# A two-block transformer forward on one core: the first shift and scale in three stages

## The chip, the cores and the metric

The kernel runs on one core of a Trainium2 chip. Time is device microseconds (us) of one execution. A core has TensorE (PE; its weight loads are listed apart as PEld), VectorE (DVE), ScalarE (ACT), GpSimd (POOL) and SyncE (SP), which here only issues transfers.

## The reference, cut to what matters

Two blocks follow each other on 256 tokens of width 1024. Everything is float32. The change touches only the start of the first block's first layer:

```python
cs = jax.nn.silu(c)
for layer in range(DEPTH):
    mod = cs @ ada_w[layer] + ada_b[layer]            # 1024 x 3072
    shift, scale, gate = jnp.split(mod, 3, axis=-1)
    h = rms_norm(x, norm_g[layer]) * (1.0 + scale[:, None, :]) + shift[:, None, :]
    ...
    y = even_mixer(h, ...)                            # first: proj = h @ w_in
    x = x + gate[:, None, :] * y
```

So shift and scale, 2048 columns of one vector times ada_w, must be there before h, and h before the first product with w_in.

## The kernel before

**Slots.** All weights stand in HBM as slots of 128 partitions by 2048 floats (1 MB). NAMES (`plan`) lists them in the order in which TensorE uses them; IDX is a name's place there. SyncE issues their transfers in the order LOADS, into a ring of four buffers (`ring`) and three more (in `big2`); a transfer into a used buffer waits until `slot_done`, which counts the slots that TensorE has finished, has passed the buffer's last user. The first slots are ada0_0 to ada0_7 (shift and scale of layer 0), then even0, even2, even4, even1, even3, even12 (EVEN_FIRST: column blocks of w_in, 256 columns each).

**An ada slot** holds 512 columns of ada_w for half of the depth (4 of 8 chunks of 128 rows). `pe_slot` multiplies it with cs, chunk by chunk, in four groups of 32 columns of the array, 16 instructions of 128 columns; two slots make one bank of PSUM. `dve_mod_slot` reduces a bank in four steps to eight columns, of which `dve_mod` makes mod: shift (columns 0 to 7, one per chunk of h) and 1 + scale times norm_g (8 to 15).

**Split products.** A product with w_in is made of three in float32r: high weights by high h, high weights by the rest of h, rest of the weights by high h. A slot's high part is a cast on ScalarE into `w_split` (two buffers, `act_highs`), its rest a subtraction on VectorE back into the ring (`dve_lows`). h has eight chunks: `hh` (high, VectorE), `hT` (full, ScalarE) and `hT_r` (the rest, VectorE). `scr` is x over its root mean square. A slot takes 3 x 16 instructions.

**The head.** TensorE (block of L2386) multiplies ada0_0 and ada0_1, then sums the squares of x (`pe_row_squares`), then the other ada slots, with `pe_turning` between and behind them: products of constants that nothing reads. Then `pe_first_pair` multiplies even0 and even2, in the order: high by high for both, the rest of even0 by high, high of even0 by the rest of h (even0 ends), high of even2 by the rest, the rest of even2 (even2 ends). All other slots follow in order by `pe_slot`. ScalarE (L2479) squares x, takes the root, casts even0 and even2 in halves, makes hT, and then `act_slot` for each name: it empties the slot's bank, then makes the high part of the slot two behind, which needs the `w_split` buffer of the slot that has just ended. VectorE (L2588) makes scr and mod, hh, the rests.

Every engine runs its own list in order. A signal of `s` is counted by who posts it and taken by who waits.

## Time and profile before

| | us |
|---|---|
| median of 3 runs (1266.88 to 1285.79) | 1268.56 |
| profiled execution | 1268.02 |
| its span, first to last instruction | 1266.2 |
| TensorE busy | 1241.9 (98%) |
| VectorE busy | 828.0 (65%) |
| ScalarE busy | 684.1 (54%) |
| moved by DMA | 222.91 MB, mean 176 GB/s |

Busy is the time in which an engine worked on an instruction; a matmul instruction on float32 leaves two records, one on float32r leaves one. Register, branch and semaphore work is not counted. The times of the views count from the span's start.

### The profile page before, as it was taken

To read this page: it belongs to the slowest core of one execution; us is meant where nothing else is said; L and a number is where in the kernel's file an instruction comes from. 1 tells how busy PE (TensorE), PEld (TensorE's weight loads), DVE (VectorE), ACT (ScalarE), POOL (GpSimd) and SP (SyncE) were. 2 spreads that over 40 slices of the span, in tenths; PEclk is the share of its full clock that TensorE was granted. 3 is DMA by queue.
4 is the path that set the end of the run, shared out by engine and by line. 5 is a ranking of instruction groups with operands and counts; after the bars stand their busy time and mean duration, and the time that the engine had idled before them with its cause. 6 is when DMAs were issued, how large, how long until landed. Compare 5 with 4: busy or idle time off the path is not lost.

```text
span 1266.2 us, 24533 instructions
## 1 busy us (share of the span) xinstructions
PE 1241.9 (98%) x10376; PEld 1123.4 (89%) x10376; DVE 828.0 (65%) x1239; ACT 684.1 (54%) x886; POOL 99.1 (8%) x83
## 2 busy tenths in 40 slices
PE   6999999999999999999999999999999999999998
PEld 5998899879999999899888888999999999888886
DVE  3667856886866969766655545766868857555533
ACT  2556446765756567245544435756567345544433
POOL 0000000000000430230000000000430130000000
PEclk9999999999999999999999999999999999999999
DMA  9867665624544433225555554544442325555552
GB/s 383 299 259 277 253 232 189 259 100 160 168 140 167 167 134 134 70 101 176 190 172 194 185 185 168 168 159 164 152 152 101 102 100 183 177 190 189 176 170 96
DMA packets 35101, 222.91 MB, mean 176 GB/s; under 512 B 3888, under 2 KB 8240, under 8 KB 9264
## 3 DMA queue, kind: packets, MB, share of 16 engines
q1 hardware_dynamic: 31104, 215.97, 48.5%
q10 hardware_dynamic: 3888, 5.38, 1.3%
q8 instruction: 82, 1.34, 0.4%
q14 instruction: 27, 0.22, 0.0%
HBM read 220.28 MB, written 1.05 MB: 175 GB/s over the span
## 4 chain that ended last, share of the span: by engine, by line
PE 93%; DVE 3%; DMA 2%; ACT 1%; issue 1%; SPq 0%; POOL 0%; ACTq 0%; DVEq 0%
PE pj L637 62%; PE yv L637 14%; PE sc L637 10%; PE tp L637 4%; DVE ring_rounded L751 1%; PE tp L503 1%; DMA ring<-weights 1%; DMA xT<-x_t 1%; PE tp L2003 1%; DVE att_area L580 1%; ACT att_area L534 0%; ACT probsT L1669 0%; DVE att_area L605 0%; ACT w_split L742 0%; DVE big L1876 0%
## 5 line engine op out<-in xcount | busy, mean ns | idle before, releaser
L751 DVE TENSOR_TENSOR ring_rounded<-ring,w_split 128x2048 fp32r<-128x2048 f32 x106 | 248.2, 2347 | 59.5 <-ACT w_split L742 57.3
L2240 DVE TENSOR_TENSOR ring_rounded<-ring,big_rounded 128x2048 fp32r<-128x2048 f32 x66 | 151.3, 2293 | 107.4 <-ACT big_rounded L2116 107.2
L742 ACT CAST w_split<-ring 128x2048 fp32r<-128x2048 f32 x106 | 202.2, 1908 | 31.8 <-PE pj L637 22.5
L637 PE MATMUL pj<-h_split,w_split 128*128 128x256 f32 x1264 | 172.1, 286 | 0.2 <-ACT w_split L2498 0.2
L637 PE MATMUL pj<-h_split,ring_rounded 128*128 128x256 f32 x1264 | 165.3, 281 | 1.3 <-DVE ring_rounded L751 1.3
L637 PEld LDWEIGHTS pj<-h_split,w_split 128*128 128x128 f32 x1264 | 156.2, 189 | 6.3 <-issue 5.1
L637 PEld LDWEIGHTS pj<-h_split,ring_rounded 128*128 128x128 f32 x1264 | 155.7, 188 | 2.9 <-DVE ring_rounded L751 2.1
L2116 ACT CAST big_rounded<-ring 128x2048 fp32r<-128x2048 f32 x66 | 126.2, 1911 | 50.2 <-PE pj L637 44.8
L637 PE MATMUL pj<-hT_rounded,w_split 128*128 128x256 f32 x1136 | 146.0, 280 | 0.0
L637 PEld LDWEIGHTS pj<-hT_rounded,w_split 128*128 128x128 f32 x1136 | 139.2, 188 | 0.0
L637 PE MATMUL sc<-big_rounded 128*128 128x512 f32 x176 | 67.8, 391 | 0.0
L637 PE MATMUL pj<-big_rounded 128*128 128x512 f32 x176 | 67.5, 389 | 0.0
L2340 ACT ACTIVATE big<-pj 128x512 f32<-128x512 f32 x32 | 19.1, 598 | 67.5 <-PE pj L637 67.4
L534 ACT ACTIVATE att_area<-att_area,stat 128x256 f32<-128x256 f32 (+1 forms) x80 | 39.9, 499 | 19.4 <-DVE stat L580 8.3
L2125 ACT CAST big_rounded<-tp 128x512 fp32r<-128x512 f32 x22 | 12.9, 588 | 69.1 <-PE tp L2003 69.1
L637 PE MATMUL yv<-big_rounded,yT_rounded 128*128 128x512 f32 x192 | 49.2, 398 | 0.1
L637 PE MATMUL yv<-big_rounded,rw_rounded 128*128 128x512 f32 x192 | 47.7, 390 | 0.0
L637 PE MATMUL yv<-ring_rounded,yT_rounded 128*128 128x512 f32 x192 | 47.5, 389 | 0.0
L1425 POOL TENSOR_TENSOR big<-big 128x512 f32<-128x512 f32 x16 | 30.7, 1919 | 200.0 <-DVE big L1341 189.7
L637 PEld LDWEIGHTS yv<-ring_rounded,yT_rounded 128*128 128x128 f32 x192 | 36.0, 188 | 7.5
L637 PEld LDWEIGHTS yv<-big_rounded,rw_rounded 128*128 128x128 f32 x192 | 35.9, 188 | 7.4
L637 PEld LDWEIGHTS yv<-big_rounded,yT_rounded 128*128 128x128 f32 x192 | 35.0, 188 | 8.1 <-issue 0.8
(379 smaller groups left out, 2127.2 us busy)
## 6 DMA issues: line engine op xcount, KB each, us to landing
ring<-weights SPq DMA_DIRECT2D x180, 1024.0 KB, 4.9
big<-weights SPq DMA_DIRECT2D x20, 1024.0 KB, 7.8
first_block<-biases ACTq DMA_DIRECT2D x26, 192.0 KB, 4.4
first_block<-biases SPq DMA_DIRECT2D x6, 192.0 KB, 10.8
xT<-x_t SPq DMA_DIRECT2D x1, 1024.0 KB, 9.7
con<-constants SPq DMA_DIRECT2D x1, 897.0 KB, 6.6
aux<-small SPq DMA_DIRECT2D x1, 832.0 KB, 10.9
out_t<-scr SPq DMA_DIRECT2D x3, 256.0 KB, 2.4
```

Source lines behind the costliest of these rows:

```text
L503: last = nc.tensor.transpose(tp[m["t"] % 2][:, at:at + P], probs[:, m["g"] % 4, it, jt * P:(jt + 1) * P], C("ident"))
L534: ins = nc.scalar.activation(pr, pr, ACT.Exp, bias=st[:, it:it + 1], scale=-1.0, accum_out=st[:, 2 + it:3 + it])
L580: ins = nc.vector.tensor_tensor_reduce(probs[:, m["g"] % 4, it, 0:size], sc[m["g"] % 2][:, it * SEQ:it * SEQ + size], table[:, P - it * P: ...
L637: return nc.tensor.matmul(out, lhsT, rhs, start=start, stop=stop, skip_group_check=True)
L742: act.post(nc.scalar.copy(w_split[:, w % 2], ring[:, in_ring(idx)]), s["w_high"])
L751: dve.post(nc.vector.tensor_tensor(ring_r[:, at], ring[:, at], w_split[:, w % 2].bitcast(F32), ALU.subtract), s["w_low"])
L1425: pool.tell(nc.gpsimd.tensor_tensor(d, b, b[:, :, n - 1:n].to_broadcast([P, 512 // (2 * n), 2 * n]), ALU.subtract), s["hgrn_diff"])
L2003: last = nc.tensor.transpose(tp[j % 2][:, (2 * c + T) * P:(2 * c + T + 1) * P], by_token(j, T)[:, c * P:(c + 1) * P], C("ident"))
L2116: act.tell(nc.scalar.copy(w_high(i), ring[:, in_ring(w_at(t, i))]), s["ffn_high"])
L2125: act.tell(nc.scalar.copy(hidden_high(j), tp[j % 2][:, :]), s["ffn_placed"])
L2240: dve.tell(nc.vector.tensor_tensor(w_low(t, i), w, value(w_high(i)), ALU.subtract), s["ffn_low"])
L2340: free(act, nc.scalar.activation(GATES[name], b[:, :], ACT.Tanh, scale=0.5), name)
```

## The change

The list of the first slots is now ada0_0, ada0_1, ada0_4, ada0_5 (shift and scale of the first four chunks of h), four new slots, and EVEN_FIRST. A new slot, a quarter, holds 256 columns of ada_w over the full depth: ada0_22 and ada0_26 are shift and scale of chunks 4 and 5, ada0_23 and ada0_27 those of chunks 6 and 7. `pe_quarter` multiplies one with 32 instructions of 64 columns into a bank `yv`; `dve_quarters` reduces a pair of them in four steps. The transfers are in the order of HEAD_ORDER: vec, x_t, the constants, four ada slots, even0, even2, and then the four quarters. h and the products of even0 and even2 are made in three stages of 4, 2 and 2 chunks, with the quarters between them. The squares stand ahead of all ada slots, and the nine turnings behind ada0_5 are gone; the twelve ahead of the pair stay.

```diff
-HEAD_BUFFERS = [RING + i for i in range(OWN)] + list(range(RING)) + [RING]
+HEAD_BUFFERS = [RING, RING + 1, RING + 2, 0, 3, RING, RING + 1, RING + 2]
+HEAD_ORDER = [0, 1, 2, 3, 8, 9, 4, 5, 6, 7]
+HEAD_MODS = ("ada0_0", "ada0_1", "ada0_4", "ada0_5")
+HEAD_QUARTERS = (("ada0_22", "ada0_26"), ("ada0_23", "ada0_27"))
...
-LOADS = sorted(range(len(NAMES)), key=lambda i: (max(BUFFERS[i][2], i - EARLY_BY if i >= len(HEAD_BUFFERS) else -1), i))
+LOADS = HEAD_ORDER + sorted(range(len(HEAD_ORDER), len(NAMES)), key=lambda i: (max(BUFFERS[i][2], i - EARLY_BY), i))
...
+            def highs(ks):
+                for n, (name, high, _) in enumerate(slots):
+                    if ks[0] == 0:
+                        pe_open(pe, name)
+                    for k in ks:
+                        if k % 4 == 0:
+                            pe.take(s["w_high" if k else "squares"])
+                        if n == 0:
+                            pe.take(s["h_first_high"])
+                        products(name, high, hh, k, True)
+            def high_lows(ks):
...
+                        products(name, high, hT_r, k)
+            def lows(n, ks):
...
+                    last = products(name, low, hh, k, False, True)
+                if ks[-1] == KC - 1:
+                    last.then_inc(slot_done, 1)
+            highs(HEAD_STAGES[0])
+            high_lows(HEAD_STAGES[0])
+            pe_quarter(pe, HEAD_QUARTERS[0][0])
+            lows(0, HEAD_STAGES[0])
+            pe_quarter(pe, HEAD_QUARTERS[0][1])
+            lows(1, HEAD_STAGES[0])
+            pe_quarter(pe, HEAD_QUARTERS[1][0])
+            highs(HEAD_STAGES[1])
+            pe_quarter(pe, HEAD_QUARTERS[1][1])
+            high_lows(HEAD_STAGES[1])
+            for n in range(2):
+                lows(n, HEAD_STAGES[1])
+            highs(HEAD_STAGES[2])
+            high_lows(HEAD_STAGES[2])
+            for n in range(2):
+                lows(n, HEAD_STAGES[2])
+        HEAD_STAGES = (range(4), range(4, 6), range(6, 8))
...
+        def pe_quarter(pe, name):
+            idx, g = IDX[name], quarter_of(name)
+            arrived(pe.eng, idx)
+            w = weights(idx).rearrange("p (k j n) -> p k j n", k=KC, j=4)
             for k in range(KC):
+                for j in range(4):
+                    last = matmul(quarter_bank(g)[32 * j:32 * j + 32, quarter_at(g):quarter_at(g) + 64],
+                                  cs[:, k:k + 1].to_broadcast([P, 32]), w[:, k, j], k == 0, k == KC - 1)
             last.then_inc(slot_done, 1)
...
+            def act_h_first(ks):
+                act.take(s["mod_ready"])
+                for k in ks:
+                    act.post(nc.scalar.activation(hT[:, k], scr[:, k], ACT.Identity, bias=mod[:, k:k + 1],
+                                                  scale=mod[:, 8 + k:9 + k]), s["h_first"])
+            act_h_first(HEAD_STAGES[0])
             for n in EVEN_FIRST[:2]:
...
-            eng.wait_ge(s["mod_ready"].sem, 1)
-            for k in range(KC):
-                act.post(nc.scalar.activation(hT[:, k], scr[:, k], ACT.Identity, bias=mod[:, k:k + 1],
-                                              scale=mod[:, 8 + k:9 + k]), s["h_first"])
+            for stage in HEAD_STAGES[1:]:
+                act_h_first(stage)
...
+            def dve_h_first(ks):
+                dve_mod_part(dve, ks[0], ks[-1] + 1)
...
+            for n in HEAD_MODS:
+                dve_slot(dve, n)
+            dve_h_first(HEAD_STAGES[0])
+            dve_lows(dve, IDX[EVEN_FIRST[1]])
+            for pair, stage in zip(HEAD_QUARTERS, HEAD_STAGES[1:]):
+                dve_quarters(dve, pair)
+                dve_h_first(stage)
```

How the lists of the engines change is shown at three places.

SyncE, the first transfers, before (big and ring hold weight slots, con the constants):

```order
L1054 DMA vec<-vectors 128x187
L1060 DMA big<-weights 128x2048
L1054 DMA con<-constants 128x288
L1060 DMA big<-weights 128x2048
L1054 DMA xT<-x_t 128x2048
L1060 DMA big<-weights 128x2048
L1060 DMA ring<-weights 128x2048 x4
L1060 DMA big<-weights 128x2048 [waits slot_done]
L1060 DMA ring<-weights 128x2048 [waits slot_done] x4
L1057 DMA first_block<-biases 128x384 x6
L1060 DMA ring<-weights 128x2048 [waits slot_done] x3
```

and with the change:

```order
L1101 DMA vec<-vectors 128x187
L1101 DMA xT<-x_t 128x2048
L1101 DMA con<-constants 128x288
L1116 DMA big<-weights 128x2048 x3
L1116 DMA ring<-weights 128x2048 x4
L1116 DMA big<-weights 128x2048 [waits slot_done] x3
L1116 DMA ring<-weights 128x2048 [waits slot_done] x2
L1113 DMA first_block<-biases 128x384 x6
L1116 DMA ring<-weights 128x2048 [waits slot_done] x3
```

x_t goes from the fifth place to the second, even0 and even2 (two of the first four into the ring) ahead of the four quarters.

ScalarE from the casts of even0 and even2 to the cast of even4 (big is an emptied bank), before:

```order
L2498 CAST w_split<-ring 128x1024 [waits weights_landed0,norm_root]
L2498 CAST w_split<-ring 128x1024
L2498 CAST w_split<-ring 128x1024 [waits weights_landed1]
L2498 CAST w_split<-ring 128x1024
L2503 ACTIVATE hT<-scr,mod 128x256 [waits mod_ready]
L2503 ACTIVATE hT<-scr,mod 128x256 x7
L1863 ACTIVATE big<-pj 128x512 [waits slot_done]
L742 CAST w_split<-ring 128x2048 [waits slot_done,weights_landed2,bank_free0]
```

and with the change:

```order
L2550 ACTIVATE hT<-scr,mod 128x256 [waits mod_ready,norm_root]
L2550 ACTIVATE hT<-scr,mod 128x256 x3
L2559 CAST w_split<-ring 128x1024 [waits weights_landed1]
L2559 CAST w_split<-ring 128x1024
L2559 CAST w_split<-ring 128x1024 [waits weights_landed2]
L2559 CAST w_split<-ring 128x1024
L2550 ACTIVATE hT<-scr,mod 128x256 [waits mod_ready]
L2550 ACTIVATE hT<-scr,mod 128x256
L2550 ACTIVATE hT<-scr,mod 128x256 [waits mod_ready]
L2550 ACTIVATE hT<-scr,mod 128x256
L1919 ACTIVATE big<-pj 128x512 [waits slot_done]
L746 CAST w_split<-ring 128x2048 [waits slot_done,weights_landed3,bank_free0]
```

Four pieces of hT now stand ahead of the casts, and four behind them; the order of the bank of even0 and the cast of even4 is the same.

TensorE at the end of the pair (pj0 is the bank of even0, pj1 that of even2; the row of w_split,h_split is even4), before:

```order
L637 MATMUL pj0<-hT_rounded_56,w_split 128x256 [waits h_low]
L637 MATMUL pj0<-hT_rounded_56,w_split 128x256
L637 MATMUL pj1<-hT_rounded_56,w_split 128x256 x16
L637 MATMUL pj1<-h_split,ring_rounded_49 128x256 [waits w_low]
L637 MATMUL pj1<-h_split,ring_rounded_49 128x256 x15
L637 MATMUL pj0<-w_split,h_split 128x256 [waits w_high,bank_free0,weights_landed2]
L637 MATMUL pj0<-w_split,h_split 128x256 x15
```

and with the change:

```order
L641 MATMUL pj0<-hT_rounded_56,w_split 128x256 [waits h_low]
L641 MATMUL pj0<-hT_rounded_56,w_split 128x256
L641 MATMUL pj1<-hT_rounded_56,w_split 128x256 x4
L641 MATMUL pj0<-h_split,ring_rounded_49 128x256 x4
L641 MATMUL pj1<-h_split,ring_rounded_49 128x256 x4
L641 MATMUL pj0<-w_split,h_split 128x256 [waits w_high,bank_free0,weights_landed3]
L641 MATMUL pj0<-w_split,h_split 128x256 x15
```

The last products of the two slots now stand directly behind each other, where 32 products of even2 stood behind even0's last. In the middle of the pair, quarters (yv) now stand between products:

```order
L641 MATMUL pj1<-hT_rounded_56,w_split 128x256 x8
L641 MATMUL yv0<-ring,cs 32x64 [waits weights_landed3]
L641 MATMUL yv0<-ring,cs 32x64 x31
L641 MATMUL pj0<-h_split,ring_rounded_49 128x256 [waits w_low]
L641 MATMUL pj0<-h_split,ring_rounded_49 128x256 x7
L641 MATMUL yv0<-big2,cs 32x64 [waits weights_landed4]
L641 MATMUL yv0<-big2,cs 32x64 x31
L641 MATMUL pj1<-h_split,ring_rounded_49 128x256 [waits w_low]
L641 MATMUL pj1<-h_split,ring_rounded_49 128x256 x7
```

The first two quarters stand ahead of the products with the rests of even0 and of even2.

## Rows read from the trace of the kernel before

**Rows 1.** The page's first part: busy us, share of span, instructions.

```profile
PE 1241.9 (98%) x10376; PEld 1123.4 (89%) x10376; DVE 828.0 (65%) x1239; ACT 684.1 (54%) x886; POOL 99.1 (8%) x83
```

**Rows 2.** Chain of waits, first 62 us: start, us, what.

```profile
2.58 9.65 DMA xT<-x_t
...
21.81 11.14 DMA ring<-weights
...
42.02 20.02 PE pj L637 x166
```

**Rows 3.** Timeline, TensorE: start, us, engine, line, op, out<-in, count, idle before.

```profile
6.25 1.94 PE L637 MATMUL pj<-big,cs 128*32 128x128 f32 x32 [6.25 <-DMA big<-weights]
...
23.07 1.08 PE L637 MATMUL pj<-ring,cs 128*32 128x128 f32 x32 [1.32 <-DMA ring<-weights]
...
24.08 2.27 PE L637 MATMUL sc<-con 128*128 128x128 f32 x18
...
28.04 1.08 PE L637 MATMUL pj<-big,cs 128*32 128x128 f32 x32 [0.67 <-DMA big<-weights]
...
29.05 2.94 PE L637 MATMUL sc<-con 128*128 128x128 f32 x24
...
31.84 2.13 PE L637 MATMUL pj<-h_split,w_split 128*128 128x256 f32 x16
...
36.14 2.06 PE L637 MATMUL pj<-h_split,ring_rounded 128*128 128x256 f32 x16
...
38.04 3.96 PE L637 MATMUL pj<-hT_rounded,w_split 128*128 128x256 f32 x32
...
44.03 2.08 PE L637 MATMUL pj<-w_split,h_split 128*128 128x256 f32 x16
```

**Rows 4.** Timeline of VectorE and ScalarE around the pair.

```profile
20.89 3.63 DVE L2615 TENSOR_TENSOR scr<-xT,rstd 128x256 f32<-128x256 f32 x8
...
24.56 0.19 DVE L1892 CUSTOM_DVE_ANT_0 diag<-pj,con 128x32 f32<-128x32 f32 x1
...
26.31 0.08 DVE L1892 DVE_READ_ACCUMULATOR2_ANT mod_raw<- 128x1 f32 x1
...
30.25 0.18 DVE L1906 TENSOR_TENSOR mod<-mod_raw,vec 128x16 f32<-128x16 f32 x1
...
30.54 2.00 ACT L2498 CAST w_split<-ring 128x1024 fp32r<-128x1024 f32 x2 [10.00 <-DMA ring<-weights]
30.66 2.68 DVE L2622 TENSOR_SCALAR h_split<-scr,mod 128x256 fp32r<-128x256 f32 x8
...
34.88 4.04 ACT L2503 ACTIVATE hT<-scr,mod 128x256 f32<-128x256 f32 x8
...
39.67 2.29 DVE L751 TENSOR_TENSOR ring_rounded<-ring,w_split 128x2048 fp32r<-128x2048 f32 x1
...
40.14 0.60 ACT L1863 ACTIVATE big<-pj 128x512 f32<-128x512 f32 x1 [1.22 <-PE pj L637]
40.77 1.91 ACT L742 CAST w_split<-ring 128x2048 fp32r<-128x2048 f32 x1
```

**Rows 5.** Stretches, tile tp on TensorE: us, busy (count), granted clock, DMA, GB/s.

```profile
13.09:16.50 3.41, 3.41 (x8) 1.00 1.01 425
16.50:18.39 1.89, 1.89 (x9) 1.00 1.04 442
```

**Rows 6.** Timeline of the start of one slot, and all such records.

```profile
23.07 0.32 PE L637 MATMUL pj<-ring,cs 128*32 128x128 f32 x4 [1.32 <-DMA ring<-weights]
...
23.07 0.42 PE L637 MATMUL pj<-ring,cs 128*32 128x128 f32 x8 [1.32 <-DMA ring<-weights]
...
L637 PE MATMUL pj<-ring,cs x128: 272/273/296, 19.8 to 27.1; 128*32 128x128 f32 x128
```

**Rows 7.** Stretches at the end: busy by engine, the granted clock third last.

```profile
1260.40:1262.00 1.60, 0.00 (x1) 0.00 (x0) 1.33 (x3) 0.98 (x3) 0.00 (x0) 1.00 0.73 273
1262.00:1263.00 1.00, 0.00 (x0) 0.00 (x0) 0.65 (x2) 0.72 (x1) 0.00 (x0) 0.68 0.24 88
```

More of the change, by code:

```diff
@@ L868, in products @@
                 return last
-            one, two = names
-            (high_one, low_one), (high_two, low_two) = map(split_of, names)
-            pe_open(pe, one)
-            for k in range(KC):
-                if k % 4 == 0:
-                    pe.take(s["w_high" if k else "squares"])
-                pe.take(s["h_first_high"])
-                products(one, high_one, hh, k, True)
-            pe_open(pe, two)
-            for k in range(KC):
-                if k % 4 == 0:
-                    pe.take(s["w_high" if k else "squares"])
-                products(two, high_two, hh, k, True)
@@ L883, in pe_first_pair @@
-            pe.take(s["w_low"])
-            for k in range(KC):
-                products(one, low_one, hh, k)
-            for k in range(KC):
-                pe.take(s["h_low"])
-                last = products(one, high_one, hT_r, k, False, True)
-            last.then_inc(slot_done, 1)
-            for k in range(KC):
-                products(two, high_two, hT_r, k)
-            pe.take(s["w_low"])
-            for k in range(KC):
-                last = products(two, low_two, hh, k, False, True)
@@ L895, in pe_first_pair @@
-            last.then_inc(slot_done, 1)
+            slots = [(name, *split_of(name)) for name in names]
+            def highs(ks):
[8 more added lines that the diff above has]
+                        products(name, high, hh, k, True)
@@ new lines, in high_lows @@
+            def high_lows(ks):
+                for n, (name, high, _) in enumerate(slots):
+                    for k in ks:
+                        if n == 0:
+                            pe.take(s["h_low"])
+                        products(name, high, hT_r, k)
+            def lows(n, ks):
+                name, _, low = slots[n]
+                if ks[0] == 0:
+                    pe.take(s["w_low"])
+                for k in ks:
+                    last = products(name, low, hh, k, False, True)
+                if ks[-1] == KC - 1:
+                    last.then_inc(slot_done, 1)
@@ new lines, in dve_quarters, with dve_mod_part @@
+        def dve_quarters(dve, pair):
+            dve.eng.wait_ge(slot_done, IDX[pair[1]] + 1)
+            for name in pair:
+                g = quarter_of(name)
+                for m in range(2):
+                    at = quarter_at(g) + 32 * m
+                    dve.do(nc.vector.tensor_tensor_reduce(diag[:, 0:32], quarter_bank(g)[:, at:at + 32], C("quad"), 1.0, 0.0,
+                                                          ALU.mult, ALU.add, mod_raw[:, 2 * g + m:2 * g + m + 1]))
+        def dve_mod_part(dve, a, b):
+            both = lambda ap: ap.rearrange("p (s c) -> p s c", s=2)[:, :, a:b]
+            dve.do(nc.vector.tensor_tensor(both(mod[:, 0:16]), both(mod_raw[:, 0:16]), both(VS("ada_b", 0, 16)), ALU.add))
+            dve.tell(nc.vector.scalar_tensor_tensor(mod[:, 8 + a:8 + b], mod[:, 8 + a:8 + b], 1.0, VS("norm_g", a, b),
+                                                    ALU.add, ALU.mult), s["mod_ready"])
@@ L2389, in _ @@
             eng.wait_ge(s["cond_ready"].sem, 1)
-            for i in range(8):
-                if i == 2:
-                    eng.wait_ge(head_landed, 16)
-                    for j in range(KC // 2):
-                        pe_row_squares(pe, j, scr)
-                    eng.wait_ge(s["lambda_terms"].sem, 1)
-                    for j in range(2):
-                        last = matmul(tp[1][:, j:j + 1], C("ones")[0:HD, :], cols[0:HD, 32 + j:33 + j])
-                    last.then_inc(s["square_sums"].sem, 1)
-                pe_slot(pe, f"ada0_{i}")
-                if i == 5:
-                    pe_turning(sc[0], 9)
+            eng.wait_ge(head_landed, 16)
+            for j in range(KC // 2):
+                pe_row_squares(pe, j, scr)
+            eng.wait_ge(s["lambda_terms"].sem, 1)
+            for j in range(2):
+                last = matmul(tp[1][:, j:j + 1], C("ones")[0:HD, :], cols[0:HD, 32 + j:33 + j])
+            last.then_inc(s["square_sums"].sem, 1)
+            for n in HEAD_MODS:
+                pe_slot(pe, n)
             pe_turning(sc[0], 12)
@@ L2783, in pack_weights @@
         for name, values in zip(numbered(f"ada{layer}_", 12), w):
-            out[IDX[name]] = values
+            if name in IDX:
+                out[IDX[name]] = values
+    for name in HEAD_QUARTERS[0] + HEAD_QUARTERS[1]:
+        w = a["ada_w"][0].reshape(KC, P, 12, 2, 4, 32)[:, :, quarter_of(name)]
+        out[IDX[name]] = w.transpose(1, 0, 3, 2, 4).reshape(P, SLOT)
     put(a["ab_w_in"][0], numbered("even", 16))
```

52 lines of the change are left out of this document (26 added, 26 removed).

## The prediction

> **What bounds the kernel now.** I read the views from coarse to fine. The page says that TensorE is busy for 98% of the span [rows 1]: whatever moves the moment from which TensorE works without a break moves the end. The chain of waits over the first 62 us [rows 2] says where that moment is made: x_t must land (until 12.23), the sums of squares follow, and then a transfer (until 32.95) whose end lets ScalarE make the high part of even2. After that the chain is TensorE alone, and the last piece, 20 us long, starts at 42.02 and has no gap. So the head counts up to the start of the third weight slot, even4, which stands at 44.03 in the timeline of TensorE [rows 3]. I compare the two kernels at that one point; behind it the order of work, the buffers' turn and the bound stay as they are, so a shift of even4 is a shift of the end.
>
> The transfers are in one queue. In before the first megabyte lands when TensorE first starts (6.25), the third (x_t) at 12.23, the seventh (ada0_5) at 23.07, the tenth (even0) at 30.54 and the eleventh (even2) at 32.95 [rows 2 to 4]; at the end about 2.47 us each.
>
> **What the change does to the transfers.** The new kernel brings the same eleven megabytes (x_t, eight parts of ada_w, two weight slots), in another order, so I give each place in the queue the time it has now: x_t first, 6.2; the four first-half slots until the fifth place, 17.7 (on the line between 12.23 and 23.07, 2.7 each); even0 20.4; even2 23.1; the quarters 22, 26, 23 and 27 at 25.5, 28.0, 30.5 and 32.95. SP waits for three slot_done counts before the last three quarters; these are reached by about 16, long before their bytes could move, so no price. Behind the quarters, even4 now waits on SP for quarter 22 being used (about 30); the queue still holds quarter 27 until 32.95, so even4 lands near 35.5 as it does now: no price either. The biases stay behind even1, and even3 behind even0's end.
>
> **The start of the pair.** In before scr (x over its root) is ready at 24.52, which is 12.3 after x_t [rows 2, 4]. With x_t at 6.2 it is ready at 18.5. This assumes that the squares on TensorE cost what they cost now: 3.41 us for the first eight records and 1.89 for the other eight [rows 5]. The four first-half slots are multiplied by 18.7 (17.7 and one slot of 1.08). VectorE then needs eight reductions (24.56 to 26.39, 1.83), two steps for mod (30.25 to 30.66, 0.41) and is at 20.8. ScalarE makes four pieces of h (half of 4.04, 2.0) and only then, by its program order, the first half of even0's high part (half of 2.00). So the pair starts at **24.0**, not when even0 lands (20.4). VectorE's high parts (0.33 each) and low corrections run beside that.
>
> **The pair itself.** A product costs 0.12 (sixteen in 1.90 from 36.14 to 38.04 [rows 3]). There are 96 of them, as before, but four quarter slots stand between them in TensorE's order. A quarter slot is not in the trace. It has 32 instructions of 64 columns where a slot of now has 16 of 128: the same columns. The nearest row, one slot, is 1.08 [rows 3]. I take 1.15: a slot's steady 0.87 (eight groups of four in 0.11, 0.42 less 0.32 for the second group [rows 6]) and some 0.15 for each change to and from 32-wide tiles (behind the slot of 23.07 the first filler starts at 24.08, not at 23.94 [rows 3]). Lower bound 0.6, if half the columns made a group twice as cheap; upper bound 2.16, if each of the now 64 records costs what one of 32 costs now (1.08 / 32 = 34 ns).
>
> Step by step from 24.0: even0's first products until 25.0; even2's wait for its first half, two casts later (25.9), until 26.9; 16 corrections until 28.8; quarter 22 until 29.95; low products of even0 30.9; quarter 26 32.05; those of even2 33.0 (the low tiles, two of 2.29 on VectorE from 25.0, are ready by 29.6); quarter 23 34.15. h 4 and 5 need four reductions, two mod steps and one high part after quarter 26: in before 29.12 to 31.07, with the wait to TensorE 2.05 [rows 3, 4], so 34.1: just in time. Products of stage two until 35.1, quarter 27 (landed at 32.95) until 36.25, corrections and low products until 38.2; stage three may start at 36.25 + 2.05 = 38.3 and takes 24 products, until 41.2. **even0 ends four products before that, at 40.75, where it ended at about 39.97 (38.04 + 16 products).**
>
> What is late next is the price of the new order. In before even0 ended 4 us ahead of even2, so ScalarE emptied its bank (40.14) and made even4's high part (40.77 to 42.68) under even2's products: TensorE waited for nothing at 44.03. Now both weight slots end together, and the same two steps stand bare: 2.8 from the end of even0 to even4's first product (39.97 to 42.68, and 0.1). So even4 starts at 40.75 + 2.8 = 43.55, against 44.03: **0.5 us earlier.** The pair begins 7.8 us earlier (31.84 [rows 3] to 24.0) and gives 7.3 back: 4.6 to the quarters, 0.9 to the wait for even2's cast, the rest to this last wait, less the short waits of now.
>
> The profiled execution took 1268.0 us (span 1266.2), half a microsecond under the median shown. The sum is 1268.0 - 0.5 = **1267.5 us**. With the bounds of single terms it is 1266.5 to 1269.
>
> The price of a quarter is the weakest term. Four records of a slot are over 0.32 after the first begins, and one alone takes 0.27 [rows 6]: the four start within 0.05, so up to there no record has a start of its own to pay; the second four add 0.10, which is 27 ns a record or 0.8 ns a column. Which of the two readings holds for half the columns, no row shows. The Trainium skill ("TensorE: Matmul & The Clock Gate", section "Wait — 56ns, not 53.3ns?") states that start-to-start never drops below about 25 ns however small a matmul is. By that rule the 64 records of a quarter would take at least 1.6, an estimate from that page, and the sum would be near rival 3; the four starts within 0.05 speak against it in this trace.
>
> **The rivals.**
> 1. *The last transfer sets the end after all* (15%). If quarters are cheap (0.6) and the pair starts earlier, TensorE catches up with the queue: 32.95 + 1.15 + 2.05 + 20 products (2.4) = 38.55 for even0, 41.35 for even4: 2.7 earlier, **1265.3**. For it: the transfers are on the chain now. Against: ScalarE's casts follow its h.
> 2. *The clock falls before the pair* (25%), slower than before. The twelve fillers now start at 18.7 and end at 21.6 (2.94 [rows 3]); then TensorE has nothing for 2.4 us. At the kernel's end it stopped at 1260.4, and the clock mean of 1262 to 1263 is 0.68 [rows 7], so it fell from 2.4 to 1.2 GHz some 2 us after the stop. An idle 1.32 at 23.07 did not cost it [rows 3]. When cold, it took 3.41 us of work to come back [rows 5], at half speed. A first 0.95 of loss hides in the wait for even2's cast; what is left is 0.75 to 2.9, I take 2: **1269.5**. It decides if the fall comes inside the gap, that is if the gap is over about 2 us at the wrong moment.
> 3. *Records, not columns, price a quarter* (15%), slower: 2.16 for 1.15, four times, +4.0, all on TensorE's path: **1271.5**. It decides above 1.3 us a quarter. The page named above would have it so; the four starts within 0.05 [rows 6] are why it has no more.
> 4. The forecast, a serial chain of TensorE and ScalarE: 45%.
>
> That the change does not do what it says is no rival here: the order of each engine shows it.
>
> **The numbers.** The forecast's own range (1266.5 to 1269) has 45%. From 1265.2 to 1271.3 the first two rivals are in too, and the third, with the tails, is left out: about 80%. 2% of this kernel is 25 us, which is about what a measurement can tell from no change; the whole head before even4 is 44 us and no case moves more than 5. Faster by over 2%: 1%; within 2%: 97%; slower: 2% (a wait that I missed).
>
> **What would show it.** In the new profile: x_t landing near 6.2 and scr's last piece at 18.5; the pair's first product at 24 right after ScalarE's first half cast; quarter 27 begun near 35, over 1.5 us after its landing; a gap on TensorE of about 2.3 before even4, put down to the cast; even4 at 43.5. The forecast is wrong if quarter 27 starts on its landing (rival 1), if the first sixteen products take over 0.2 each (rival 2), or if a quarter takes over 1.5 (rival 3).

## The result, and the profile of the changed kernel

The changed kernel takes 1271.84 us (median, 1270.99 to 1273.51), the kernel before 1266.9: **0.4% slower, ratio 1.0039 [1.0028, 1.0049]**. I had forecast 1267.5 and a range to 1271.3, so the time lies above the range and the sign was wrong. The profiled execution took 1271.62 with a span of 1269.8, 3.6 more than before (1266.2). even4, the point at which I compared the two, starts at 47.79 instead of 44.03 [rows 3]: +3.8. The whole difference of these two profiles is made in the head, as the method assumed (a second profile of the kernel before, experiment 12, limits this); the head itself came out 4.24 later than the 43.55 of the forecast.

TensorE is busy for as long as before (1241.9 [rows 1]): the time went into waiting. From the first and the third part of the changed kernel's page (busy us, share and instructions; packets, MB and share of a queue):

```profile
PE 1241.1 (98%) x10486; PEld 1122.6 (88%) x10486; DVE 828.6 (65%) x1243; ACT 684.1 (54%) x886; POOL 99.1 (8%) x83
...
q8 instruction: 83, 1.36, 0.4%
```

The chain of waits of the changed kernel up to 62 us (start, us, what) answers to [rows 2]:

```profile
1.18 4.91 DMA xT<-x_t
...
6.95 6.16 PE tp L641 x16
...
23.60 2.84 ACT w_split L2559 x3
...
26.57 4.16 PE pj L641 x24
30.73 1.03 PE yv L641 x64
...
37.24 0.95 PE yv L641 x57
38.19 1.98 issue
40.17 0.32 PE yv L641 x7
40.49 4.61 PE pj L641 x36
45.12 0.61 ACT big L1919
45.74 1.91 ACT w_split L746
...
47.79 14.32 PE pj L641 x119
```

One transfer is left in it, x_t; the one of even2, 11.14 long before, is gone, and quarters (yv) stand in it instead. The odd piece is "issue" for 1.98: TensorE stands in the middle of a quarter, 57 records done and 7 to go, and waits for nothing that the profile shows. The timeline of TensorE answers to [rows 3]:

```profile
17.88 2.94 PE L641 MATMUL sc<-con 128*128 128x128 f32 x24
24.79 1.41 PE L641 MATMUL pj<-h_split,w_split 128*128 128x256 f32 x8 [3.96 <-ACT w_split L2559]
26.57 2.05 PE L641 MATMUL pj<-h_split,w_split 128*128 128x256 f32 x8 [0.37 <-ACT w_split L2559]
28.42 2.31 PE L641 MATMUL pj<-hT_rounded,w_split 128*128 128x256 f32 x16
30.66 1.10 PE L641 MATMUL yv<-ring,cs 128*32 128x64 f32 x64
...
36.02 1.22 PE L641 MATMUL pj<-h_split,w_split 128*128 128x256 f32 x8
...
47.79 2.15 PE L641 MATMUL pj<-w_split,h_split 128*128 128x256 f32 x16 [2.23 <-ACT w_split L746]
```

Eight products take 2.05 at 26.57; at 36.02 eight are over in 1.22. The stretches say why; the granted clock, as a share of 2.4 GHz, is the third number from the end:

```profile
24.80:26.00 1.20, 1.20 (x8) 1.10 (x8) 0.48 (x1) 1.20 (x2) 0.00 (x0) 0.83 0.99 410
26.00:27.00 1.00, 0.63 (x3) 0.46 (x3) 1.00 (x1) 1.00 (x2) 0.00 (x0) 0.50 1.06 426
28.00:28.50 0.50, 0.50 (x4) 0.50 (x4) 0.50 (x1) 0.00 (x0) 0.00 (x0) 0.50 0.88 361
29.00:30.00 1.00, 1.00 (x11) 1.00 (x10) 1.00 (x1) 0.00 (x0) 0.00 (x0) 1.00 1.02 426
```

0.50 is the 1.2 GHz level. TensorE had stopped at 20.8 and begun again at 24.79; the clock fell after that idle, when the products were already running, and came back by 29.

The stop stands in the list of what TensorE waited for (us in total, times, longest):

```profile
PE yv L641 <- issue: 2.0, 1, 2.0
...
PE tp L641 <- issue: 0.9, 1, 0.9
```

The second one is in the first attention, at 521, and the first profile of the kernel before has one there too; I come back to it.

### The profile page after: what moved, and what is told of

It reads as the page before. It is cut to its first block, busy times and chain, and to the rows that moved or that the text cites. A ratio compares the mean times of both kernels' runs of the same rounds, so it can differ in the third digit from the quotient of the medians.

```text
span 1269.8 us, 24755 instructions
## 1 busy us (share of the span) xinstructions
PE 1241.1 (98%) x10486; PEld 1122.6 (88%) x10486; DVE 828.6 (65%) x1243; ACT 684.1 (54%) x886; POOL 99.1 (8%) x83
## 3 DMA queue, kind: packets, MB, share of 16 engines
q8 instruction: 83, 1.36, 0.4%
## 4 chain that ended last, share of the span: by engine, by line
PE 91%; DVE 4%; ACT 3%; issue 2%; DMA 0%; POOL 0%; ACTq 0%; SPq 0%; DVEq 0%
PE pj L641 60%; PE yv L641 14%; PE sc L641 10%; PE tp L641 4%; DVE ring_rounded L755 2%; PE tp L507 1%; PE tp L2059 1%; ACT w_split L746 1%; DVE att_area L584 1%; DMA xT<-x_t 0%; ACT att_area L538 0%; DVE scr L2672 0%; ACT probsT L1725 0%; DVE att_area L609 0%; ACT w_split L2559 0%
```

## The experiments

Every edit is to the changed kernel unless it says otherwise. The kernel before ran beside them at 1266.86 to 1267.72 (medians).

**1. Longer fillers ahead of the pair.**

```diff
-            pe_turning(sc[0], 12)
+            for _ in range(12):
+                matmul(sc[0][:, 0:288], C("ident"), con[:, 0:288])
```

> The twelve fillers ahead of the pair are 288 columns wide instead of 128: as many instructions, 5.8 us of work instead of 2.9, so that TensorE is busy from 17.9 to about 23.7. Theory (clock): the low clock from 25.6 to 29.0 of the changed kernel was the price of the idle 4 us ahead of the pair; here the clock column stays at 1.00 from 20 to 30, the 24 products from 26.57 to 30.73 take 2.9 to 3.1 instead of 4.16, and even4 starts 1.0 to 1.3 earlier, at about 46.6; the time falls by about 1.2. Rival (the later wait sets the end anyway): the clock stays up but even4 starts at 47.8 as before, because the 2 us stop of TensorE in quarter 27 only becomes longer.

Measured: 1272.57 (1272.38 to 1272.76), ratio to before 1.0043 [1.0028, 1.0058]; no gain, and even4 starts at 48.43. Its timeline and two of its stretches:

```profile
27.12 1.19 PE L641 MATMUL pj<-h_split,w_split 128*128 128x256 f32 x8 [0.60 <-ACT w_split L2560]
...
39.45 0.32 PE L641 MATMUL yv<-big,cs 128*32 128x64 f32 x7 [1.77 <-issue]
39.69 1.72 PE L641 MATMUL pj<-hT_rounded,w_split 128*128 128x256 f32 x8
41.21 1.91 PE L641 MATMUL pj<-h_split,ring_rounded 128*128 128x256 f32 x8
```

```profile
25.00:29.00 4.00, 3.07 (x24) 2.92 (x25) 2.94 (x2) 2.93 (x4) 0.00 (x0) 1.00 1.02 420
...
40.10:43.50 3.40, 3.40 (x18) 3.40 (x18) 2.61 (x14) 1.09 (x2) 0.00 (x0) 0.51 0.34 122
```

With the idle ahead of the pair cut from 3.96 to 1.50, the clock stays up in the pair (eight products in 1.19 instead of 2.05). It does so in runs 1, 2, 3 and 11, all with these longer fillers, and it fell there in the three profiles with idles of 3.96 to 4.47 (the changed kernel, 4 and 6), so idle time was the cause of that fall. But the stop in quarter 27 stayed, and here the clock fell behind it. One loss was exchanged for the other.

**2. The same filling with 64 records more.** It asks where the stop sits: at an instruction, at a time, or at a count of records.

```diff
-            pe_turning(sc[0], 12)
+            for _ in range(28):
+                matmul(sc[0][:, 0:123], C("ident"), con[:, 0:123])
```

> As e1_fill, but 28 fillers of 123 columns instead of 12 of 288: the same time, 64 more instruction records on TensorE. Theory (supply of instructions): the stop in quarter 27 comes where TensorE has used up the instructions that were brought to it, so it stands at a fixed count of records (952 weight loads and matmuls from the start); with 64 more ahead it comes 64 records earlier in the work: about 25 matmul records into quarter 27 instead of 57. Rival (something of quarter 27 itself: its transfer, its bank): the stop stays behind the 57th matmul record of quarter 27, or is gone in both.

Measured: 1269.54 (one run), even4 at 46.20. This is 2.3 below the changed kernel and 3.0 below run 1, though the stop (1.82) is there: the clock did not fall behind it, nor in the wait before even4.

```profile
34.00:47.00 13.00, 8.94 (x171) 8.26 (x160) 5.15 (x21) 5.52 (x8) 0.00 (x0) 1.00 0.68 250
```

The stop came after 25 matmul records of quarter 27 instead of 57: 32 matmuls and their 32 loads sooner, as many as the fillers had added. The stretches from the start to the stop, of the changed kernel, of run 1 and of this one, count the records (the numbers with x; matmuls, then weight loads):

```profile
0.00:38.20 38.20, 26.42 (x477) 23.18 (x477) 19.23 (x65) 14.37 (x21) 0.94 (x9) 0.96 0.91 362
```

```profile
0.00:37.67 37.67, 28.42 (x477) 23.92 (x477) 19.23 (x65) 14.38 (x21) 0.94 (x9) 1.00 0.91 367
```

```profile
0.00:36.34 36.34, 27.30 (x477) 24.38 (x477) 19.22 (x65) 14.38 (x21) 0.93 (x9) 1.00 0.94 374
```

477 and 477 in all three, at three different times, and in runs 4, 5 and 7 as well. The stop belongs to a place in TensorE's instruction stream, not to quarter 27, its data or its landing. I take it for the supply of instructions. The page lists a queue that brings them, with 83 packets of 16 KB (1.36 MB). TensorE has 20,972 matmul and load records and, in the trace, 327 of its sequencer (nearly all semaphore waits): about 64 bytes a record, 256 records a packet. In the changed kernel one packet moved between 37.60 and 38.80, and none from there until 41.40:

```profile
q8 instruction: 1, 0.02, 4.9%
```

The counts of all stops bear this out. With the sequencer's 7 records the stop stands behind 961 in all six. The second stop of the changed kernel, at 521, stands behind 5007 matmuls, 5007 loads and 163 records of the sequencer:

```profile
0.00:521.20 521.20, 500.84 (x5007) 467.20 (x5007) 367.88 (x740) 310.13 (x467) 34.81 (x35) 1.00 0.56 204
```

That is 10,177, and 10,177 - 961 is 36 times 256. The profiles of this study have 19 such stops, from 0.37 to 1.98; each stands at 961 plus a multiple of 256, the edge of a packet, and TensorE goes on 1.3 to 1.6 after a packet has landed (here 38.66 and 40.17). At none of these edges, with a stop or without, does its work begin sooner than 1.27 after the packet for it has landed. So the supply is the cause. Why the packet came so late there, no run shows: it began to move when 31 records were left, where most packets begin with about 260 left.

The Trainium skill ("Runtime: NRT & Kernel Launch", section "Instruction fetch mechanics") says that instructions come in blocks of 16 KiB, 256 of them, fetched while the block before is executed, and that crossing a block's edge is mostly hidden. This trace agrees with the size, and with "mostly": the list of waits has two such stops against 83 packets, but the first cost 1.98.

**3. Quarters of half the depth** (with the fillers of 1). The other half of each sum is left out, so a quarter has half the records and half the work.

```diff
-            for k in range(KC):
+            for k in range(KC // 2):
...
```

> As e1_fill, but each quarter slot is multiplied over the first half of its depth only (16 instructions instead of 32; the other half of that sum is left out, so shift and scale of the chunks 4 to 7 are not the reference's). Theory (supply of instructions): 256 records fewer between the two fetches, so TensorE is no longer ahead of its supply and the 2 us stop is gone; even4 starts 2.0 earlier for the stop and at most 2.0 for the halved work of four quarters against e1_fill, so about 43 to 44.5. Rival (a stop of quarter 27 itself): a stop of 1 to 2 us stays and even4 starts 2 earlier at most.

Measured: 1268.25 (one run). No stop, even4 at 43.06; run 6 below tells the records from the work. The clock fell at the end of the next idle, the wait of 2.24 for even4's cast: 43.00 to 46.00 at 0.50, and even4's first sixteen products took 3.52 instead of 2.15.

**4. even0 finished first, twenty products of even2 held back for the wait.** In `pe_first_pair`:

```diff
...
-            high_lows(HEAD_STAGES[0])
+            high_lows(HEAD_STAGES[0], (0,))
...
-            highs(HEAD_STAGES[2])
-            high_lows(HEAD_STAGES[2])
-            for n in range(2):
-                lows(n, HEAD_STAGES[2])
+            highs(HEAD_STAGES[2], (0,))
+            high_lows(HEAD_STAGES[2], (0,))
+            lows(0, HEAD_STAGES[2])
+            high_lows(HEAD_STAGES[0], (1,))
+            highs(HEAD_STAGES[2], (1,))
+            high_lows(HEAD_STAGES[2], (1,))
+            lows(1, HEAD_STAGES[2])
```

> The changed kernel, with even0 finished ahead of even2: 20 products of even2 (its corrections of stage one and all of its stage three) stand behind the last one of even0. Theory (the bare wait): emptying even0's bank and the cast for even4, 2.8 us, now run beside 2.4 us of products, so the wait of 2.2 to 2.4 before even4 falls to under 0.6 and even4 starts about 2 earlier than in the changed kernel, at about 45.8; the time falls by about 2. Rival (the order only moves the wait): TensorE idles as much inside the pair, waiting for h, and even4 starts within 0.5 of 47.8.

Measured: 1271.33 (1269.28 to 1273.14), ratio to before 1.0035 [1.0023, 1.0048]. In its profile the wait is filled:

```profile
45.61 2.15 PE L641 MATMUL pj<-w_split,h_split 128*128 128x256 f32 x16 [0.35 <-ACT w_split L746]
```

even4 starts 2.18 earlier, as expected, and the profiled run (1269.28) is 2.3 below that of the changed kernel; but it is the quickest of six, and the median moved only 0.5. The stop (1.64) and the fall in the pair are in this profile too. What the other runs lost cannot be seen in it, but their mean granted clocks are on record: 0.998 in the two quickest (1269.28 and 1270.13), 0.995 or 0.996 in the four others. So these had the clock low for longer; where, is not shown.

**5. ScalarE in the order of need**: even0's first half is cast ahead of h, even2's first half ahead of even0's second (`act_half` casts half of a slot).

```diff
...
-            act_h_first(HEAD_STAGES[0])
-            for n in EVEN_FIRST[:2]:
-                ...
+            arrived(eng, IDX[EVEN_FIRST[0]])
+            act_half(EVEN_FIRST[0], 0)
+            act_h_first(HEAD_STAGES[0])
+            arrived(eng, IDX[EVEN_FIRST[1]])
+            act_half(EVEN_FIRST[1], 0)
+            for n in EVEN_FIRST[:2]:
+                act_half(n, 1)
...
```

> The changed kernel with ScalarE's order alone changed: the first half of even0's high part ahead of the first four pieces of h, then the first half of even2's, then the two second halves. Theory (ScalarE's order sets the start): even0 lands near 20, so its first half is there before h, and even2's first half is done one cast (0.95) earlier than now; the second group of eight products starts about 1.9 earlier than 26.57, near 24.7, and TensorE's gap ahead of the pair shortens to under 2 us, so the clock may stay up. even4 starts 1 to 3 earlier than 47.8. Rival (the transfers set the start): even2's first half waits for its landing and the second group starts within 0.5 of 26.57.

Measured: 1272.93 (one run). The pair starts 2 us earlier and gains nothing:

```profile
22.83 1.68 PE L641 MATMUL pj<-h_split,w_split 128*128 128x256 f32 x8 [1.89 <-DVE h_split L2686]
25.43 2.05 PE L641 MATMUL pj<-h_split,w_split 128*128 128x256 f32 x8 [0.93 <-ACT w_split L2556]
27.28 3.44 PE L641 MATMUL pj<-hT_rounded,w_split 128*128 128x256 f32 x16
30.65 1.10 PE L641 MATMUL yv<-ring,cs 128*32 128x64 f32 x64
```

The clock was low from 23.6 to 30.4, through nearly all of the 32 products, so quarter 22 starts at 30.65, as in the changed kernel (30.66). It fell again behind the stop, and even4 starts at 49.02, 1.2 later than there. I had expected that the clock might stay up with under 2 us of idle ahead of the pair; it fell with 1.89.

**6. The later slots repacked**: a pair of slots still holds the same 512 columns, but each slot has all 512 for half of the depth, so that it takes 16 instructions of 128 columns instead of 32 of 64.

```diff
...
-            for k in range(KC):
+            for k in range(4):
+                at = 4 * (g >= 6) + k
                 for j in range(4):
-                    last = matmul(quarter_bank(g)[32 * j:32 * j + 32, quarter_at(g):quarter_at(g) + 64],
+                    last = matmul(quarter_bank(g)[32 * j:32 * j + 32, 0:P], cs[:, at:at + 1].to_broadcast([P, 32]),
...
```

> The changed kernel with the four later slots packed anew: each pair holds the same 512 columns (shift and scale of two chunks), but a slot has all 512 for half of the depth, so it is multiplied by 16 instructions of 128 columns instead of 32 of 64. Same bytes, same columns, half the instruction records (64 instead of 128 a slot). Theory (supply of instructions): the stop of 2.0 us is gone, a slot of these takes 0.9 to 1.1 as before, and even4 starts about 2 earlier than in the changed kernel, at 45.8 (with the clock's fall at 25 still in it). Rival (the stop is the price of quarter 27's place, or of the transfers beside it): a stop of over 1 us stays and even4 starts within 0.7 of 47.8.

Measured: 1270.9 (1270.34 to 1271.66), ratio to before 1.003 [1.0019, 1.0041]. A slot takes 1.02 from start to start, as the quarter did with twice the records (30.66 to 31.69, 1.03), and there is no stop. even4 starts at 45.76, 2.03 earlier. Then part of it is lost again: the clock fell behind the wait before even4 (46.50 to 49.70 at 0.50; its first sixteen products in 3.28).

**7. TensorE kept busy from the start**: six products of constants ahead of the squares.

```diff
+            eng.wait_ge(s["constants_set"].sem, 1)
+            for _ in range(6):
+                matmul(sc[0][:, 0:SEQ], ones256[:, 0:P], ones256[:, :])
             eng.wait_ge(s["cond_ready"].sem, 1)
```

> The changed kernel with six products of constants, 256 columns wide, on TensorE from 1.7 on, ahead of the squares of x, and nothing else. Theory (the squares are slow because they are TensorE's first work): the 16 records of the squares take 3.5 to 5.2 instead of 6.15, h and the pair start 1 to 2.5 earlier than 24.8, unless the fourth ada slot (landed at 16.9, 1.1 of work, eight reductions) then sets the start: not under 22.5. Rival: the squares are paced by ScalarE's squaring of x and take about 6 all the same.

Measured: 1271.23 (one run).

```profile
7.15 3.69 PE L641 MATMUL tp<-scr,con 128*128 128x256 f32 x16 [0.55 <-ACT scr L776]
...
22.57 3.83 PE L641 MATMUL pj<-h_split,w_split 128*128 128x256 f32 x16 [1.96 <-ACT w_split L2562]
```

The squares take 3.69 instead of 6.15 and the pair starts 2.2 earlier. The clock then fell at its start (0.50 from 23 to 26) and behind the wait before even4 (46.90 to 50.00), and the stop of 1.98 stood at the same count of records.

**8. All of it**: the edits of 5, 6 and 7, 6 fillers of 288 columns, and even0 ahead in the pair:

```diff
...
-            highs(HEAD_STAGES[0])
-            high_lows(HEAD_STAGES[0])
+            highs(HEAD_STAGES[0], (0,))
+            high_lows(HEAD_STAGES[0], (0,))
+            highs(HEAD_STAGES[0], (1,))
+            high_lows(HEAD_STAGES[0], (1,))
...
+            lows(0, HEAD_STAGES[2])
+            highs(HEAD_STAGES[2], (1,))
+            high_lows(HEAD_STAGES[2], (1,))
...
```

> All remedies together: slots of e7_halves; ScalarE's order of e5_casts; in TensorE's order even0's corrections ahead of even2's first products and even0's stage three wholly ahead of even2's; six fillers of 288 columns ahead of the pair; six products of constants, 256 columns wide, from 1.7 on, so that the clock is up when the squares of x start at 6.9. By the theories (start of the pair, clock, supply, bare wait) the squares take 3.5 to 5 instead of 6.1, the pair starts at 21 to 22, the last quarter begins within 1 us of its landing (33), and even4 starts at 40.4 to 42: 2 to 3.5 earlier than in the kernel before (44.03), a ratio of 0.997 to 0.9985. Rival (the clock falls in the gaps that the transfers leave): one fall of 3.4 us costs up to 1.7 and the gain is under 1.5.

Measured: **1265.02 (1264.7 to 1266.54), ratio to before 0.9984 [0.9975, 0.9993]**: quicker than both kernels. In the profiled run (1266.40) even4 starts at 42.42, 0.4 past the bound that I had expected, and the clock still fell once, in the idle ahead of the fourth ada slot:

```profile
18.70 1.91 PE L641 MATMUL pj<-ring,cs 128*32 128x128 f32 x32 [3.10 <-DMA ring<-weights]
20.54 3.98 PE L641 MATMUL sc<-con 128*128 128x288 f32 x12
24.14 1.32 PE L641 MATMUL pj<-h_split,w_split 128*128 128x256 f32 x8
```

**9. The same with that idle bridged.**

```diff
             for n in HEAD_MODS:
+                if n == HEAD_MODS[-1]:
+                    for _ in range(6):
+                        matmul(sc[0][:, 0:288], C("ident"), con[:, 0:288])
                 pe_slot(pe, n)
```

> The run that beat both kernels (repacked slots, ScalarE's halves in the order of need, even0 ahead, warm start) with six more products of constants (288 columns) ahead of the fourth ada slot, where TensorE was idle for 3.10 us and the clock then fell from 18.8 to 22.2. Theory (idle time of TensorE makes the clock fall and so the run's spread): the clock stays up until the pair, the fourth ada slot takes 1.1 instead of 1.9, the pair starts 0.5 to 0.9 earlier than 24.14 and even4 near 41.8 instead of 42.42; the runs lie within 0.7 us of each other, median 1264.2 to 1264.8. Rival (behind the start the transfers of the later slots or ScalarE's list set the end): even4 stays at 42.2 or later and the median within 0.3 of 1265.0. Second rival: the fall moves to the next idle (the wait before even4) and the time is 1265.5 to 1267.

Measured: **1264.92 (1264.35 to 1265.31), ratio to before 0.998 [0.9972, 0.9989]**.

```profile
18.30 1.08 PE L641 MATMUL pj<-ring,cs 128*32 128x128 f32 x32
19.30 3.18 PE L641 MATMUL sc<-con 128*128 128x288 f32 x12
22.11 1.32 PE L641 MATMUL pj<-h_split,w_split 128*128 128x256 f32 x8
...
40.93 2.15 PE L641 MATMUL pj<-w_split,h_split 128*128 128x256 f32 x16 [1.31 <-ACT w_split L746]
```

The clock is 1.00 from 6 to 47, and the pair starts 2.0 earlier than in the profile of 8, more than the 0.9 I had allowed: at low clock the fillers themselves had held it up. The runs lie within 1.0 instead of 1.8 (0.7 was expected). The median hardly moved (1264.2 to 1264.8 was expected), so most runs of 8 will not have had that loss; its profile is of one of its longer runs.

**10. The kernel before with the six early products alone.**

```diff
+            eng.wait_ge(s["constants_set"].sem, 1)
+            for _ in range(6):
+                matmul(sc[0][:, 0:SEQ], ones256[:, 0:P], ones256[:, :])
             eng.wait_ge(s["cond_ready"].sem, 1)
             for i in range(8):
```

> The kernel before with one thing added: six products of constants on TensorE from about 1.75 us, ahead of its first slot, as in the run that beat both kernels. Theory (that run's gain comes from the order of the head, not from a warm start alone): the squares get shorter (16 records in 3.7 to 4.5 us instead of 5.3), but the pair of the kernel before starts on the cast of even0, which lands at 30.5, so even4 stays at 44.0 +- 0.2 and the time at 1266.9 +- 0.4. Rival (the gain is the warm start): the time falls by 1 us or more, to 1265.9 or less.

Measured: 1267.36 against 1267.22, ratio 1.0001 [0.9992, 1.001]. The squares take 3.69, but nothing waits for them there. In the profiled run, the slowest of the eleven (1268.36), the clock fell at 21 instead (idles of 1.59 and 1.41 between ada slots), the pair started at 33.20 and even4 at 44.74, 0.5 past my bound. The gain of 8 and 9 is not the early products by themselves.

**11. The two cures together**: the fillers of 1 and the slots of 6, nothing else.

```diff
...
+                at = 4 * (g >= 6) + k
...
-            pe_turning(sc[0], 12)
+            for _ in range(12):
+                matmul(sc[0][:, 0:288], C("ident"), con[:, 0:288])
...
```

> The changed kernel with both cures that were tried apart: the longer fillers (288 columns) ahead of the pair, and the later slots repacked into 16 instructions of 128 columns. Theory (the miss is the sum of the clock's fall before the pair and the stop in quarter 27, and each cure alone only moved the loss to the next idle): no stop, no fall before the pair, even4 at 45.0 to 45.5 (48.43 with the fillers alone, less the stop of 1.77 and about 1.5 of low clock behind it). The wait before even4 stays at 2.2, so the clock may fall there as it did with repacked slots: sixteen products of even4 in 3.3 instead of 2.15, and the median 1269.8 to 1270.4 with that, 1268.6 to 1269.2 without. Rival (the two losses are one, and either cure gives what there is to have): even4 at 45.7 or later.

Measured: 1268.94 (1268.55 to 1269.34), ratio to before 1.0011 [1.0001, 1.002].

```profile
25.12 1.19 PE L641 MATMUL pj<-h_split,w_split 128*128 128x256 f32 x8 [0.77 <-ACT w_split L2561]
26.90 1.19 PE L641 MATMUL pj<-h_split,w_split 128*128 128x256 f32 x8 [0.59 <-ACT w_split L2561]
...
44.77 2.15 PE L641 MATMUL pj<-w_split,h_split 128*128 128x256 f32 x16 [2.23 <-ACT w_split L746]
```

No stop and no fall: even4 at 44.77, 3.02 ahead of the changed kernel, and the median 2.90 below. Each cure alone gave +0.7 and -0.9 (medians of 1 and 6). This is the run that settles most of the miss.

**12. The kernel before, profiled again.**

> The kernel before, unchanged, profiled a second time. Its runs lie in two groups, near 1266.6 and near 1268.2, and its profile above is one of the upper group; behind even4 the spans of all profiles differ by 0.4 us at most. Theory (the two groups differ in the head, by the clock): a run of the lower group has even4 at 42.5 to 43.0 instead of 44.03 and shorter squares or products ahead of it; a run of the upper group has it at 44.0 again. Rival (the groups differ behind the head): even4 at 44.0 with a span of 1265.

Measured: 1266.44, span 1264.7. My theory fell: even4 starts at 43.83, only 0.2 earlier than in the first profile, and the other 1.3 lie behind the head. The first profile of before has a row in TensorE's list of waits that the second does not have,

```profile
PE tp L637 <- issue: 1.0, 1, 1.0
```

and in its chain of waits, in the first attention, where 64 x 64 matmuls follow each other:

```profile
517.13 0.96 issue
```

It stands at the edge of a packet, like the one in quarter 27 (experiment 2). Eleven of the 14 profiles have such a stop in the first attention, two (2 and 10) have it near 996 instead, 0.4 to 1.0 long; only this one has none. For this edge the packet landed at 516.67 in the first profile, and TensorE went on at 518.09; in the second it had landed at 513.62, and the work behind the edge began at 516.59 without a stop. So the two executions differ in when the packet came. Why it came 3 us later in the one, no run shows.

So 1.0 of those 1.3 is this stop (the rest I did not place). It also limits the method. Against this second profile the changed kernel's is 5.1 longer: 3.96 up to even4 and 1.2 behind it, where it has its stop of 0.9. The first profile of before is of one of its longer executions (1268.02); that its shorter ones, and so its median, lack the stop, only this one profile shows. If they do, it explains most of why the medians differ by 4.9 and the two first profiles by 3.6. The premise of my expectation, that the spans behind even4 differ by 0.4 at most, was wrong too: they run from 1221.5 to 1223.8 in the profiles that I had.

## Why the prediction was wrong, step by step

The miss at even4, 47.79 - 43.55 = 4.24, is read off the chain above (the first row is part of the second; the others add up):

| Step | forecast | measured | miss |
|---|---|---|---|
| x_t lands | 6.2 | 6.1 | -0.1 |
| first product of the pair | 24.0 | 24.79 | +0.8 |
| from there to even2's first product | 1.9 | 1.78 | -0.1 |
| these 8 products and 16 corrections | 2.9 | 4.16 | **+1.3** |
| quarter 22 to quarter 27 | 6.3 | 6.51 | +0.2 |
| quarter 27 | 1.15 | 3.25 | **+2.1** |
| from there to even0's end | 4.5 | 4.63 | +0.1 |
| even0's end to even4 | 2.8 | 2.67 | -0.1 |

**The step that failed** is quarter 27: I priced what a quarter costs TensorE to execute (1.15 for the columns, 2.16 if records decide) and never asked whether its instructions arrive in time. The price was right for the work: 1.03 from start to start for each of the first three, and 0.95 + 0.32 for this one, with a stop of 1.98 between. No term and no rival had it. Repacking the slots to half the instructions (6) takes the stop away and leaves the work at 1.02. The hint was in the profile that I had: its list of waits has one "issue" of 1.0 on TensorE, in the first attention. I did not use that row because it lies far behind the head. Without the stop the forecast would still have been too early, by the clock's 1.3 and the start's 0.8.

**The clock** (rival 2, 25%) came true beside the forecast's own chain: the 24 products took 1.26 more, inside the 0.75 to 2.9 worked out for it (I took 2). The place was not as I had it: the clock fell not inside the gap, some 2 us after TensorE's stop, but between 24.80 and 26.00, in the first products. That the price fits is in part luck. I forecast an idle of 2.4 and still gave the fall one chance in four. The idle was longer (3.96) since the fillers ended 0.8 earlier and the pair began 0.8 later. Runs 1 and 11 show it: shorten the idle with work and the fall is gone.

**The start**: the squares took 6.15 where I took 5.3 [rows 5]; 0.8 of the 1.5 that I had named as its bound. Run 7 shows the other end, 3.69. The change need not be the reason: in the second profile of the kernel before they took 6.12. I had taken one execution's number for the kernel's.

**The base and the method**: the sum started from 1268.0, one execution; the median of all runs of the kernel before is 1266.9. And a shift of even4 was the whole shift of the end only between executions that have the stop in the first attention; against the second profile of before 1.2 of the loss lies behind even4 (12).

**What held**: the transfers are off the path (quarter 27 landed at 32.41 and began at 37.17, as said over 1.5 later), so rival 1 is wrong. Quarters cost by columns, so rival 3 is wrong, and that the time lies near its 1271.5 is chance: 64 records in 1.03 are 16 ns each. Only quarter 27 took over 1.5, the sign named for rival 3, and not by its records' price. By the rule of the Trainium skill ("TensorE: Matmul & The Clock Gate", section "Wait — 56ns, not 53.3ns?"), at least 25 ns apart, they would have taken at least 1.6, an estimate from that page; in this trace, with four groups of 32 columns side by side, it does not hold. (By that estimate the forecast's sum would have been 1269.3, and not near rival 3, as the prediction has it.) The bare wait before even4 came as forecast (2.8, measured 2.67). And run 11, with both losses cured and nothing else changed, puts even4 at 44.77: the forecast's 43.55 with 1.12 for its later start (25.12 instead of 24.0) is 44.67. So the chain of the forecast describes the change without those two losses, and even so it gains nothing (1.0011 [1.0001, 1.002]): the pair begins 7 us earlier and gives it back to the quarters and the wait, as the prediction said.

**Why one cure alone did little.** Three idles stand in the new head: before the pair (3.96), the stop (1.98) and the wait before even4 (2.23). Each of them was followed by 1.2 GHz in one profile or another. With the first cured the clock fell behind the stop (1); with the stop cured it fell in the pair as before, and behind the wait (6). But it need not: in run 2, with the first cured, it stayed up behind both others, and in run 11 behind the wait, with the same 2.23 of idle. Why it was spared there stays open, so what one cure gives is in part luck.

## What to carry to other kernels

Price a new stretch by three things and not one: the time of its work, whether its instructions arrive in time (the list of waits said "issue" where they did not), and the idle time that it opens on TensorE, since the clock can fall after it and the next work then runs at half speed (0.50 from 26.00 to 28.50 here). Work started earlier than its partners can follow was worth nothing here; 7 us of earlier start became a loss of 4.9, and it took the edits of run 9 to make a gain of 2.3 of it. Profile the baseline twice: one execution's stop or slow squares are not the kernel's. And when a cure gives nothing, look in its profile for the same loss one idle further on before dropping the theory.

## What the runs showed that I had not expected

- TensorE stops 1.6 to 2.0 us at a fixed count of its records (477 loads and 477 matmuls from the start) in six kernels whose work there differs. With half the records in each later slot there is none (3, 6, 8, 9, 11).
- All 19 such stops stand at 961 records plus a multiple of 256, the edge of a 16 KB packet, and end 1.3 to 1.6 after one has landed.
- A stop of the same kind separates two executions of the kernel before: 0.96 at 517 in one, none in the other, where the packet had landed 3 us sooner.
- In four groups of 32 columns a matmul record of 64 columns costs half of one of 128: 1.03 a quarter by 64 records, 1.02 a slot by 32.
